# Triangular inverse on compact 64x64 diagonal blocks and per-token normalisation sums, in a two-layer decoder trunk

## The reference

```python
kk = kk / jnp.maximum(jnp.sqrt(jnp.sum(kk * kk, axis=-1, keepdims=True)), 1e-12)   # a head has 64 channels
def step(S, inp):
    sa = -jnp.einsum('bhvk,bhk->bhv', S, kk_t)
    S = (S * w_t[:, :, None, :] + sa[..., None] * (kk_t * a_t)[:, :, None, :]
         + v_t[..., None] * k_t[:, :, None, :])
    return S, jnp.einsum('bhvk,bhk->bhv', S, r_t)
mu_y = jnp.mean(y, axis=-1, keepdims=True)
var_y = jnp.mean(jnp.square(y - mu_y), axis=-1, keepdims=True)
y = ((y - mu_y) * lax.rsqrt(var_y + RWKV_GN_EPS)).reshape(B, T, RWKV_WIDTH)
...
y = conv(z) + conv_b;  return silu(layernorm(y))          # the convolution's half
```

## Time and profile before

| | us |
|---|---|
| median of 3 runs (lowest to highest) | 1399.83 (1395.85 to 1402.48) |
| profiled execution, its own time | 1401.22 |
| its span in the profile | 1399.4 |
| PE / DVE / POOL / ACT busy | 1286.4 / 713.1 / 518.6 / 425.6 |
| mean granted PE clock | 0.96 of full |
| RWKV and convolution part of layer 1 | about 600 to 1000 us of the span |

### The profile page before, as it was taken

How to read it: one execution, slowest core, us unless ns; L and a number is a source line. 1 busy time by engine, 2 the same in 40 slices (tenths; PEclk the granted TensorE clock), 3 DMA queues, 4 the chain that set the end, 5 groups by cost and what they waited for, 6 DMA issues and landing times.

```text
span 1399.4 us, 20615 instructions
## 1 busy us (share of the span) xinstructions
PE 1286.4 (92%) x8420; PEld 1038.8 (74%) x8420; DVE 713.1 (51%) x1012; ACT 425.6 (30%) x536; POOL 518.6 (37%) x374
## 2 busy tenths in 40 slices
PE   5899999999999999979798887777799999999997
PEld 4797978888888888856565666564588888888885
DVE  7336354542124444476858888686745421245333
ACT  4537333221122222253334324222432211222120
POOL 4241434555445555431121020110145544455441
PEclk9899999999999999989999998898999999999998
DMA  4321213222322223210011010000032223222321
GB/s 182 114 91 61 69 56 117 91 90 93 111 97 90 90 92 111 98 61 31 32 37 55 3 61 2 31 32 1 7 114 91 90 95 115 91 90 90 99 82 60
DMA packets 16803, 105.65 MB, mean 75 GB/s; under 512 B 1872, under 2 KB 2144, under 8 KB 4832
## 3 DMA queue, kind: packets, MB, share of 16 engines
q1 hardware_dynamic: 16304, 104.03, 21.7%
q10 hardware_dynamic: 432, 0.64, 0.1%
HBM read 102.57 MB, written 2.10 MB: 75 GB/s over the span
## 4 chain that ended last, share of the span: by engine, by line
issue 50%; PE 27%; POOL 21%; DVE 1%; DMA 0%; POOLq 0%; ACT 0%; SPq 0%; DVEq 0%
PE ps L844 23%; POOL w_lo L487 21%; PE ps L925 3%; PE ps L894 1%; DMA w_raw<-in_weights 0%; DVE x L1311 0%; PE ps L875 0%; POOL w_lo L476 0%; POOLq L481 0%; PE ps L851 0%; ACT w_hi L587 0%; POOLq L484 0%; SPq L440 0%; PE ps L868 0%; DVE x L1383 0%
## 5 line engine op out<-in xcount | busy, mean ns | idle before, releaser
L487 POOL TENSOR_TENSOR w_lo<-w_raw,w_hi 128x512 fp32r<-128x512 f32 x368 | 509.8, 1415 | 838.3 <-ACT w_hi L500 292.3
L844 PE MATMUL ps<-h_hi,w_hi 128*128 128x512 f32 x696 | 286.7, 412 | 11.8 <-POOL w_lo L476 11.8
L844 PE MATMUL ps<-h_lo,w_hi 128*128 128x512 f32 x696 | 275.4, 396 | 0.0
L844 PE MATMUL ps<-h_hi,w_lo 128*128 128x512 f32 x696 | 275.0, 395 | 0.0
L844 PEld LDWEIGHTS ps<-h_hi,w_hi 128*128 128x128 f32 x696 | 133.0, 191 | 53.4 <-issue 14.1
L575 ACT ACTIVATE w_hi<-w_raw 128x2048 fp32r<-128x2048 f32 x50 | 95.7, 1914 | 194.7 <-PE ps L844 143.4
L844 PEld LDWEIGHTS ps<-h_hi,w_lo 128*128 128x128 f32 x696 | 133.1, 191 | 28.9
L844 PEld LDWEIGHTS ps<-h_lo,w_hi 128*128 128x128 f32 x696 | 133.4, 192 | 28.2 <-issue 2.7
L844 PE MATMUL ps<-f_hi,w_lo 128*128 128x512 f32 x384 | 149.4, 389 | 0.0
L844 PE MATMUL ps<-f_hi,w_hi 128*128 128x512 f32 x384 | 149.4, 389 | 0.0
L844 PE MATMUL ps<-f_lo,w_hi 128*128 128x512 f32 x384 | 149.4, 389 | 0.0
(11 more groups left out here) (300 smaller groups left out, 1984.2 us busy)
## 6 DMA issues: line engine op xcount, KB each, us to landing
w_raw<-in_weights SPq DMA_DIRECT2D x93, 1024.0 KB, 4.9
outT<-x SPq DMA_DIRECT2D x8, 256.0 KB, 2.0
x<-in_xT SPq DMA_DIRECT2D x6, 256.0 KB, 7.7
masks_f<-in_masks SPq DMA_DIRECT2D x1, 768.0 KB, 11.0
x<-in_xT ACTq DMA_DIRECT2D x2, 256.0 KB, 6.1
w_raw<-in_weights SPq DMA_DIRECT2D x1, 512.0 KB, 6.6
low_w<-in_low_w SPq DMA_DIRECT2D x1, 512.0 KB, 11.7
sgu_ln<-in_sgu_ln SPq DMA_DIRECT2D x1, 512.0 KB, 3.5
```

The lines of the kernel that those rows point to most:

```text
L487: piece = pool.tensor_tensor(w_lo[:, j, at], w_raw[:, j, at], w_hi[:, j, at].bitcast(f32), SUB)
L844: mm = pe.matmul(bank(gb(g) if isinstance(i, int) else g % 2), w, r, start=(k == 0 and m == 0), stop=(k == K - 1 and m == 2))
```

## The change

Six things are changed.

1. `X`, `XT`, `TX` (128x8x128) become `xc`, `xtc`, `txc` (128x8x64): only the two 64x64 diagonal blocks of each system are kept, one on partitions 0 to 63, the other on 64 to 127. Levels 1 to 5 run on these, as matmuls of 64 rows by 64 by 32 columns, one on each diagonal quadrant.
2. The correction of XT gets a step of its own, `dxt`, after both halves of `dx`: 16 matmuls, then one COPY_PREDICATED over all eight systems. tx of the next level waits for X alone (`x_upd`), its dx for XT.
3. Level 6 is done on the off-diagonal 64x64 block only, and ACT rather than DVE puts the 128x128 XT together (two copies of the diagonals, two of the corner).
4. Key norm and output norm: the sums are taken for tokens on partitions (four matmuls with 2 columns), so that root, maximum and reciprocal work on 128x8 (`k_norm`, `y_norm`); eight matmuls with a broadcast stationary operand (`of_head`) spread the result back over a bank (new steps `kn` and `post` 3), from which DVE multiplies. `post` has five parts instead of four: the new part 3 spreads y's norm in level 4, and the old part 3 is now part 4, still in level 6.
5. The LayerNorm of the convolution likewise: 16 matmuls of 1 column instead of 4 of 512, root and reciprocal on 128x4, four matmuls to spread.
6. The RMS norms spread `rrms` by broadcast, without `diag`.

```diff
-        + [(f"lvl{a}{lv}", 64, 4) for lv in range(LEVELS) for a in ("X", "XT")]:
+        + [(f"lvlX{lv}", 32, 4) for lv in range(LEVELS - 1)] + [(f"lvlXT{lv}", 32, 8) for lv in range(LEVELS - 1)]:
...
+        HEAD_SUMS = BLK[:, 0:P:64]
+        def of_head(t, n, h2):
+            return t[:, n, h2:h2 + 1].broadcast_to([P, 64])
+        def tx_bank(lv, b):
+            return (2, 3)[b] if lv % 2 else (4, 5)[b]
+        def x_bank(lv, b):
+            return (4, 5)[b] if lv % 2 else (2, 3)[b]
+        def xt_bank(lv):
+            return tx_bank(lv, 0)
...
-                for i, lv in enumerate((1, 2, 3, 6)):
+                for i, lv in enumerate((1, 2, 3, 4, 6)):
...
-                end[4] += [("ks_v", c + 1), ("decay_v", c + 1, 2)]
+                end[4] += [("ks_v", c + 1), ("decay_v", c + 1, 2), ("kn", c + 1), ("kn_v", c + 1)]
...
+                if lv < LEVELS - 1:
+                    ORDER1 += [("dxt", c, lv)]
...   (ACT)
             def ks(c):
-                act.activation(t_f[:, :], bank(6), ACT.Sqrt).then_inc(s("knorm_done"), 1)
+                act.activation(k_norm[:, :, :], bank(6, 0, 2 * TT).rearrange("p (n h) -> p n h", h=2),
...
+            def dx(c, lv, b):
+                if lv < LEVELS - 1:
+                    return
+                if b == 0:
+                    act.wait_ge(s("xt_upd"), 5 * c + 5)
+                    act.activation(XT[0:64, :, 0:64], xtc[0:64, :, :], ACT.Copy).then_inc(s("xt_diag"), 1)
+                    act.activation(XT[64:128, :, 64:128], xtc[64:128, :, :], ACT.Copy).then_inc(s("xt_diag"), 1)
+                act.wait_ge(s("dx_mm"), 12 * c + 10 + b + 1)
+                act.activation(XT[0:64, 4 * b:4 * b + 4, 64:128],
...   (PE)
-                for t in range(TT):
-                    pe.wait_ge(s("diag_done"), 4 * m + t + 1)
-                    mm = pe.matmul(bank(6, t * P, t * P + P), ONES, diag[:, t, :], start=True, stop=True)
+                    mm = pe.matmul(bank(6, t * P, t * P + P), of_tokens(rrms, t), IDENT, start=True, stop=True)
...
             def ks(c):
-                pe.matmul(bank(6), BLK, t_f[:, :], start=True, stop=True).then_inc(s("ksum_done"), 1)
+                for n in range(TT):
+                    mm = pe.matmul(bank(6, 2 * n, 2 * n + 2), t_f[:, n * P:n * P + P], HEAD_SUMS, start=True, stop=True)
+            def kn(c):
+                pe.wait_ge(s("knorm_done"), c + 1)
+                pe.wait_ge(s("kn_step"), 2 * c + 2)
+                for n in range(TT):
+                    for h2, r in enumerate(COLUMN_HALVES):
+                        mm = pe.matmul(ps[r, 6, n * P:n * P + P], of_head(k_norm, n, h2), IDENT, start=True, stop=True)
...
+                        for r in COLUMN_HALVES:
+                            mm = pe.matmul(as2(ps[r, tx_bank(lv, b), 32 * at:32 * at + 32], B), SC[r, yy, r],
+                                           side_of_one(xc, r, yy, B, 0), start=True, stop=True)
...
+            def dxt(c, lv):
+                pe.wait_ge(s("tx_done"), (6 * c + lv - 1) * 2 + 2)
+                for yy in range(8):
+                    for r in COLUMN_HALVES:
+                        mm = pe.matmul(as2(ps[r, xt_bank(lv), 32 * yy:32 * yy + 32], B), txc[r, yy, :],
+                                       side_of_one(xtc, r, yy, B, 1), start=True, stop=True)
...   (DVE)
-                ts(t_f[:, :], t_f[:, :], 1e-12, None, ALU.max).then_inc(s("kn_step"), 1)
-                dve.reciprocal(t_f[:, :], t_f[:, :]).then_inc(s("kn_step"), 1)
-                stt(t_f[:, :], kx[:, :], col("k_k", c), t_f[:, :], MUL, MUL).then_inc(s("kk_done"), 1)
+                ts(k_norm[:, :, :], k_norm[:, :, :], 1e-12, None, ALU.max).then_inc(s("kn_step"), 1)
+                dve.reciprocal(k_norm[:, :, :], k_norm[:, :, :]).then_inc(s("kn_step"), 1)
+            def kn(c):
+                dve.wait_ge(s("kn_mm"), c + 1)
+                stt(t_f[:, :], kx[:, :], col("k_k", c), bank(6), MUL, MUL).then_inc(s("kk_done"), 1)
```

More of the change, by code:

```diff
@@ L200, in build @@
             om_mu = sb("om_mu", [P, 14])
+            k_norm = sb("k_norm", [P, TT, 2])
+            y_norm = sb("y_norm", [P, TT, 2])
+            c_norm = sb("c_norm", [P, TT])
         ps = ctx.enter_context(nc.psum_tensor("ps", [P, 8, 512], f32))
@@ L1244, in post @@
                     pe.wait_ge(s("ysq_done"), c + 1)
-                    pe.matmul(bank(7), BLK, ysq[:, :], start=True, stop=True).then_inc(s("yvar_mm"), 1)
+                    for n in range(TT):
+                        mm = pe.matmul(bank(7, 2 * n, 2 * n + 2), ysq[:, n * P:n * P + P], HEAD_SUMS, start=True, stop=True)
+                    mm.then_inc(s("yvar_mm"), 1)
                 if i == 3:
+                    pe.wait_ge(*post_step("yrs", c))
+                    pe.wait_ge(s("ysd_done"), c + 1)
+                    for n in range(TT):
+                        for h2, r in enumerate(COLUMN_HALVES):
+                            mm = pe.matmul(ps[r, 7, n * P:n * P + P], of_head(y_norm, n, h2), IDENT, start=True, stop=True)
+                    mm.then_inc(s("yn_mm"), 1)
+                if i == 4:
                     pe.wait_ge(s("low_act"), 2)
-                    pe.wait_ge(s("ysd_done"), c + 1)
+                    pe.wait_ge(*post_step("yn", c))
                     pe.matmul(bank(7), low_w[0:96, 1, c * P:c * P + P], low1[0:96, :], start=True, stop=True)\
@@ L1258, in conv_ln @@
                 if i == 2:
-                    for c in range(CT):
-                        pe.wait_ge(s("csq_done"), c + 1)
-                        pe.matmul(bank(5), ONES, (t_a, t_b, t_d, t_e)[c][:, :], start=(c == 0), stop=(c == CT - 1))\
-                          .then_inc(s("cvar_mm"), 1)
+                    pe.wait_ge(s("csq_done"), CT)
+                    for n in range(TT):
+                        for c in range(CT):
+                            mm = pe.matmul(bank(5, n, n + 1), (t_a, t_b, t_d, t_e)[c][:, n * P:n * P + P], ONES[:, 0:1],
+                                           start=(c == 0), stop=(c == CT - 1))
+                    mm.then_inc(s("cvar_mm"), 1)
+                if i == 3:
+                    pe.wait_ge(s("csd_done"), 1)
+                    pe.wait_ge(s("conv_step"), CT + 1)
+                    for n in range(TT):
+                        mm = pe.matmul(bank(5, n * P, n * P + P), of_tokens(c_norm, n), IDENT, start=True, stop=True)
+                    mm.then_inc(s("cn_mm"), 1)
             def out_(t, a, b):
@@ L1774, in m @@
                 tt(M_LO1[k], M_SRC1[k], F(M_HI1[k]), SUB).then_inc(s("m_lo_done"), 1)
-            steps = {"stat": start, "spread": started, "evac_a": evac_a, "evac_b": evac_b, "decay_v": decay, "ks_v": ks, "dyn": dyn, "bonus": bonus, "scores": scores,
-                     "dx": dx, "st": st, "post_v": post, "taps": taps, "conv_ln": conv_ln, "m": m}
+            steps = {"stat": start, "spread": started, "evac_a": evac_a, "evac_b": evac_b, "decay_v": decay, "ks_v": ks, "kn_v": kn, "dyn": dyn, "bonus": bonus, "scores": scores,
+                     "dx": dx, "dxt": dxt, "st": st, "post_v": post, "taps": taps, "conv_ln": conv_ln, "m": m}
             for name, *a in ORDER1:
@@ L1866, in _masks @@
     put("reset128", t % P != 0)
-    for lv in range(LEVELS):
-        B = 1 << lv
-        pair = (np.arange(64) // B)[None, :]
-        put(f"lvlX{lv}", (p // (2 * B) == pair) & (p % (2 * B) >= B))
-        put(f"lvlXT{lv}", (p // (2 * B) == pair) & (p % (2 * B) < B))
+    for lv in range(LEVELS - 1):
+        B, q = 1 << lv, p % 64
+        pair = (np.arange(32) // B)[None, :]
+        put(f"lvlX{lv}", (q // (2 * B) == pair) & (q % (2 * B) >= B))
+        put(f"lvlXT{lv}", (q // (2 * B) == pair) & (q % (2 * B) < B))
     return m
```

170 lines of the change are left out of this document (103 added, 67 removed).

## The result

The changed kernel took 1403.99 us, median of 7 runs (1401.86 to 1408.57), the kernel before on the same chip 1398.91 (1395.85 to 1402.48): a ratio of 1.0034, 95% interval 1.002 to 1.0048. Forecast were 1381 and a range of 1365 to 1397. The time is that of rival 2 (1403), which had 0.09.

What follows compares the result with a forecast made beforehand. The levels were taken as held by DVE's queue in places, elsewhere by the chain PE, ACT, PE, DVE. Pairs, tail and RMS norms summed to -18.5 us, 1401.22 to 1382.7, less 1.4 to the median: 1381, range 1365 to 1397.

Steps and rivals of the forecast that it cites:

- rival 2: Levels: PE's clock falls, 2.8 us a level; at half of 24 levels +22 - 18.5, total 1403; chance 0.09.
- the sum: All pairs, tail and RMS norms, taken by what ends last: -18.5 us together, to 1381; chance 0.57.
- PE in the levels: Levels' tx, dx and dxt: 32 columns cost the same as 64, the old 1.0 us each, no gain.
- rival 4: Levels: narrow matmuls cost half, 28 us less on PE, half of it where PE ends last: 1367; chance 0.11.
- Rival 3: Levels: matmuls on the two quadrants don't run together, 2.8 us more in each of 20 levels: 1418; chance 0.03.
- Rival 1: Each spread and its wait cost 1.5 us more, 12 in all; pairs 0 and 1 gain nothing: 1394; chance 0.20.
- Copies: DVE in the levels: smaller COPY_PREDICATED, about 0.75 us a level instead of 1.35 (2.3 at level 1); 17 us less.
- Reciprocals: DVE: nine 128x512 reciprocals of 3.35 us go, 30 us; the 128x8 ones replacing them taken at 0.15.
- Key spread: Pairs 0 to 2, before level 5's tx: 0.9 to 1.7 us wait, 1.1 work, 2 to 2.8 a pair.
- Spreads and pair ends: Spreads add 10 us of PE; ahead of pair 0 -0.5, pairs 0 to 3 -3.9, -1.0, -6.2, -5.7 us.
- Waits after the scan: PE's waits for DVE's copies after the scan in pairs 0 and 1 stay at 4 to 5 us.
- Tail: After pair 3: two reciprocals go, but LayerNorm sums wait for squares and ACT ends the chain; -0.2 us, at most -3.

Runs made afterwards that it cites:

- experiments 12: Changed kernel with the long waits in pairs 0, 1 and 3 and ahead of the key spreads filled with 28 unread matmuls: 1385.66 us, 0.9903.
- 14: Kernel before with its eight longest waits for the copy of XT filled with 49 unread matmuls: 1393.99 us, 0.9959.
- wide levels: Changed kernel with tx, dx and dxt moving 64 columns instead of 32: 1386.91 us, 0.9925; with the old normalisations as well: 1384.97 us, 0.9885.
- wide filled: Changed kernel with 64 moved columns in all levels and its long waits filled with unread matmuls: 1376.77 us, 0.9836.
- experiment 11: Changed kernel with pair 3's wait of 1.81 us ahead of tx at level 3 filled with four unread matmuls: 1.0019.
- experiment 3: Changed kernel with the old normalisations, so compact levels of 32 columns alone: 1387.38 us, 0.9927 to the kernel before.

## Why the prediction was wrong

- **The step that failed** is the cost of the clock, which the sum leaves out and rival 2 holds at 0.09. Its ground was "the lower level follows idleness already": from the mean of 0.88 to 0.92 I took that less waiting means more clock. Half of that is right, and experiments 12 and 14 show it. What it left out is the width of the matmuls that follow: with 32 columns a stretch that begins at a wait of 1.8 us runs on through four levels, with PE 92% busy (32.61 of 35.30); with 64 it was over 4 us after it began. Rival 2 priced it at +22; PE is busy 22.3 us longer, and width alone gives 15 to 17 back. By the timeline twelve of the 24 levels run at the lower level in whole or in part (two, three, three and four in pairs 0 to 3), and rival 2 "decides from ten levels on". Its mechanism is borne out. That its time is met to 1 us is in part luck, since it stands on a sum whose parts are wrong, as below.
- **PE in the levels**, no gain from half the columns: right. 32 records take 1.10 to 1.13 us at full clock with 32 columns, 1.10 to 1.15 with 64, and 1.90 to 1.92 at half clock, so rival 4 (half the cost) is out.
- **Rival 3**, two quadrants that don't run together: out by the same rows; by its price they would take 1.9 at full clock. The runs of 1.9 in the changed kernel are not that: the same code takes 1.12 up to 926 us, and projection matmuls beside the slow runs take 0.63 instead of 0.40. The rule of the Trainium skill, TensorEngine Tiling (Array Packing), section Gotcha 1: PSUM Pressure, that different row tiles can't use one PSUM bank at the same time, is not seen at work in these rows: both quadrants write to one bank at the old pace (1.12 us for 32 records against 1.16).
- **Rival 1**, the new waits eat the gain (1394): they are a part of it. On wide levels the normalisations on tokens cost 5.6 us against the old ones, where the sum had them gain.
- **Copies**, 17 us of DVE: DVE's groups of the changed kernel, 632 to 1005 us, by shape (busy, mean ns, idle before):

```profile
L1805 DVE COPY_PREDICATED xc<-masks,ps 128x128 f32<-128x128 uint8 x40 | 12.2, 322 | 37.5 <-PE ps L1259 37.4
L1811 DVE COPY_PREDICATED xtc<-masks,ps 128x256 f32<-128x256 uint8 x20 | 9.8, 489 | 10.3 <-PE ps L1269 10.1
...
L1840 DVE RECIPROCAL y_norm<-y_norm 128x8 f32<-128x8 f32 x4 | 0.8, 196 | 0.1
L1737 DVE RECIPROCAL k_norm<-k_norm 128x8 f32<-128x8 f32 x3 | 0.6, 203 | 0.1
```

  22.0 us busy against 42.9 in the earlier trace rows, 21 less for 17 costed. The compact levels as a whole (copies, new order, level 6 and narrow matmuls) gave what the change had to give: 10 to 11 us without fill, and with the clock held 0.9959 - 0.9844, 16 us (19 at 64 columns). What each of the four gave was not separated.
- **Reciprocals**, 30 us of DVE: gone (0.20 us each now), and worth nothing, or less, in all three rows of the table. In pair 2 the waits of 3.77 and 2.21 gave way to 1.16 at y's spread and 1.53 at the keys', plus two spreads; I had costed that pair as -6.2 by following DVE; it came to -2.7, with its last three levels in part or whole at the lower clock (L1337 ends at 850, and from there to the end of the pair tx, dx and dxt take up to 1.92).
- **Key spread**: the wait was forecast at 0.9 to 1.7 and is 0.93, 1.53 and 1.53; ahead of pair 0 it is 4.10, where I let the tiles cover it (-0.5, bounds -3 and +1). The spread was costed at 1.1 us and takes 1.98 at half clock. The forecast had "2 to 2.8 us a pair" for wait and work. No run has the spread without the rest; the keys' change as a whole, with its reciprocals gone, cost 5 us on wide levels and 15 on narrow ones.
- **Spreads and pair ends.** The levels end at 690.7, 787.4, 871.3 and 954.0 against 692.7, 787.3, 873.9 and 951.1: -2.0, +0.1, -2.6, +2.9. Forecast were -4.4, -5.4, -11.6 and -17.3. Taken apart, the part ahead of pair 0 gave 3.0 us (tx starts at 646.4 against 649.4), where the forecast had 0.5 and 3 as its bound; pairs 0 to 3 came to +1.0, +2.1, -2.7 and +5.5 against -3.9, -1.0, -6.2 and -5.7.
- **Waits after the scan**, forecast as still 4 to 5 us: 4.53 in pair 0, 2.64 in pair 1.
- **Tail**, -0.2: the convolution's 32 records of one column, costed at 3.6 us, took 6.9 at half clock (975.31 to 982.2), behind a wait of 1.05 for the last squares. The old ones (L1261) took 3.7 at full clock from 973.07 on, with no wait ahead. From the levels' end to the end of the profile the changed kernel loses 1.3 us, where tail and RMS norms were to give 1.2.
- **With the clock held** the sum seems nearly right: wide filled against before filled is 0.9836 - 0.9959, -17.2 us against -18.5. That is luck, since its parts are wrong both ways: the compact levels carry all of it, the reciprocals none. The changed kernel itself, filled, gains 0.9903 - 0.9959, 8 us.
- **Two sums** don't come out as written: pair 3's terms add to 5.3, not 5.7, and the chance of faster to 0.73, not 0.71. Neither changes the outcome.
- The forecast's test, "I am wrong if the levels' clock falls to 0.7", is met: 0.63 in pair 3, 0.77 and 0.78 in the others. Window 300 to 600 is unchanged, as forecast, and PE's waits for the copies at tx of levels 5 and 6 of pair 2 are gone, though it now waits 1.53 us at the key spread ahead of level 5.

## What to carry to other kernels

Where PE works in bursts between waits, halving the columns that its small matmuls move can lengthen the kernel: at 64 by 64 stationaries the narrow ones took the same time each and kept PE at 1.2 GHz for whole stages. Read the granted clock of the stage first; if it is under 1, price every edit at both levels, and try a few filler matmuls (their result unread) in the longest waits and wider moving operands before anything finer. Look at all executions, too: here a profile was up to 9 us from its kernel's median, and the granted clock went with it. A reciprocal taken off an engine that is 85% busy gave nothing where each came back as a wait and a spread on the engine that had become the bound.

## What was unexpected of the hardware

The level fell with no idle time just ahead of it (experiment 11, at 932.4 us, in a run of 32 records that follows on the one before), and it stayed down over 20 us of work with hardly a gap, most of it matmuls of 32 columns. The Trainium skill, TensorE: Matmul & The Clock Gate, section Why this matters for your kernels, advises to leave no long idle gaps between bursts; experiments 12 and 14 agree (18 and 6 us). But by that rule alone pair 3 of experiment 11 would have stayed at full clock, which its rows contradict. What in the narrow matmuls keeps the level down was not separated further: width and the 64-row stationaries came together, and only the width was changed by itself. The 2-column sums are not needed for it: pair 3 of experiment 3 has none, and its levels run at 0.63 as well.
